# Expert rows gathered by quarters and turned by VectorE two tiles ahead, in a decoder layer with a grouped mixture of experts

## The reference, cut to what matters

```python
def chunk_fn(args):
    xc, gc = args
    h = jax.nn.silu(jnp.einsum('cd,edf->cef', xc, w_gate)) * jnp.einsum('cd,edf->cef', xc, w_up)
    h = h * gc[:, :, None].astype(h.dtype)
    return jnp.einsum('cef,efd->cd', h, w_down)
```

## Time and profile before

| | |
|---|---|
| median of 3 runs | 1026.58 us (1020.91 to 1030.8) |
| profiled execution | 1020.71 us; its span 1018.7 us |
| mean granted TensorE clock, whole span | 0.956 of full |
| TensorE matmuls | 909.4 us busy (89%) |
| VectorE | 687.5 us (67%) |
| ScalarE | 561.0 us (55%) |
| GpSimd | 366.0 us (36%) |
| expert tiles | from about 533 to 976 us of the span |

### The profile page before, as it was taken

The page is one execution under the profiler, slowest core; times in us unless marked ns, Lnnn a source line. Parts: engine busy times, 40 slices in busy tenths (PEclk is TensorE's granted clock), DMA queues, the critical chain, the costliest instruction groups (busy, mean ns, idle before and its releaser), DMA issues.

```text
span 1018.7 us, 15879 instructions
## 1 busy us (share of the span) xinstructions
PE 909.4 (89%) x4802; PEld 712.9 (70%) x4803; DVE 687.5 (67%) x1017; ACT 561.0 (55%) x804; POOL 366.0 (36%) x238
## 2 busy tenths in 40 slices
PE   6999999999897899999918999999999999999920
PEld 5877888644465567888717888888887888888710
DVE  4339888896999945737697748798888734314326
ACT  4256576787686665702334646777777634323323
POOL 0000089999999990000000212213323211111116
PEclk9999999999799999999959999999999999999965
DMA  8550111000000100433565889999999897433264
GB/s 232 128 144 21 42 42 63 1 1 1 1 2 1 43 1 22 156 124 148 234 249 207 294 285 313 405 382 404 399 388 405 305 352 226 125 65 99 41 198 173
DMA packets 63052, 171.15 MB, mean 168 GB/s; under 512 B 19200, under 2 KB 33536, under 8 KB 50688
## 3 DMA queue, kind: packets, MB, share of 16 engines
q1 hardware_dynamic: 55664, 143.85, 38.4%
q0 software_dynamic: 7056, 25.69, 10.6%
q10 hardware_dynamic: 288, 1.05, 0.3%
HBM read 141.74 MB, written 26.21 MB: 165 GB/s over the span
## 4 chain that ended last, share of the span: by engine, by line
PE 45%; DMA 10%; DVE 6%; ACT 2%; issue 2%; POOLq 0%; POOL 0%; ACTq 0%; DVEq 0%; SPq 0%
PE ps L459 13%; PE ps L461 12%; PE ps L460 12%; DMA raw<-in_w_gate 8%; PE ps L924 2%; PE ps L797 1%; DVE wlo L1708 1%; DVE sm L1549 1%; ACT whi L1215 1%; PE ps L764 1%; PE ps L960 1%; PE ps L848 1%; DMA acc_d<-ysb,idx_add 1%; PE ps L784 1%; DVE xa L1563 0%
## 5 line engine op out<-in xcount | busy, mean ns | idle before, releaser
L1708 DVE TENSOR_TENSOR wlo<-raw,whi 128x2048 fp32r<-128x2048 f32 x96 | 216.0, 2287 | 51.2 <-ACT whi L1215 51.1
L1215 ACT CAST whi<-raw 128x2048 fp32r<-128x2048 f32 x96 | 180.4, 1912 | 47.9 <-DMA raw<-in_w_gate 18.5
L459 PE MATMUL ps<-whi,xgT_hi 128*128 128x512 f32 x384 | 152.0, 396 | 5.4 <-DVE xgT_lo L1718 5.4
L461 PE MATMUL ps<-whi,xgT_lo 128*128 128x512 f32 x384 | 149.8, 390 | 0.0
L460 PE MATMUL ps<-wlo,xgT_hi 128*128 128x512 f32 x384 | 149.5, 389 | 0.0
L1803 POOL TENSOR_SCALAR tapped<-hpad,par 128x1024 f32<-128x1024 f32 x30 | 92.0, 3067 | 3.0
L459 PE MATMUL ps<-xT_hi,w_hi 128*128 128x512 f32 (+1 forms) x224 | 87.2, 389 | 4.7 <-DVE w_lo L1304 3.0
L459 PEld LDWEIGHTS ps<-whi,xgT_hi 128*128 128x128 f32 x384 | 72.3, 188 | 21.3 <-issue 5.6
L461 PE MATMUL ps<-xT_hi,w_lo 128*128 128x512 f32 (+1 forms) x224 | 86.3, 385 | 0.0
L460 PE MATMUL ps<-xT_lo,w_hi 128*128 128x512 f32 (+1 forms) x224 | 86.3, 385 | 0.0
L1881 POOL COPY idx_now<-slot_token 128x1 int32 (+1 forms) x24 | 7.7, 319 | 218.7 <-PE ps L924 218.7
(11 more groups left out here) (305 smaller groups left out, 1825.0 us busy)
## 6 DMA issues: line engine op xcount, KB each, us to landing
raw<-in_w_gate SPq DMA_DIRECT2D x32, 1024.0 KB
raw<-in_w_up SPq DMA_DIRECT2D x32, 1024.0 KB, 12.7
raw<-in_w_down SPq DMA_DIRECT2D x32, 1024.0 KB
w_raw<-in_w_in SPq DMA_DIRECT2D x14, 512.0 KB, 4.1
x_tok<-in_x SPq DMA_DIRECT2D x8, 512.0 KB, 7.4
wo_raw<-in_w_o SPq DMA_DIRECT2D x16, 256.0 KB, 3.0
x_res<-in_x SPq DMA_DIRECT2D x16, 256.0 KB, 3.4
x_d<-xa SPq DMA_DIRECT2D x4, 512.0 KB, 6.0
```

The source lines that it names most:

```text
L459: pe.matmul(out, l_hi, r_hi, start=start, stop=False)
L461: return pe.matmul(out, l_lo, r_hi, start=False, stop=stop)
L1215: act.copy(whi[:, n, :], raw[:, n, :]).then_inc(gu_hi if n < 4 else dn_hi, 1)
L1708: dve.tensor_tensor(wlo[:, n, :], raw[:, n, :], f32(whi[:, n, :]), ALU.subtract).then_inc(gu_lo if n < 4 else dn_lo, 1)
```

## The change

Each index table entry now leads to four quarter rows. `xg` has row quarter q of 32 tokens on partitions 32q to 32q+31, and the four groups of 32 tokens of a tile lie beside each other in it: four indirect DMAs of 128 x 1 KB in place of one of 128 x 4 KB. One VectorE instruction, in 32x32 blocks, turns `xg` into `xr`, a new SBUF buffer with the layout that the eight TensorE transposes gave in PSUM. `xr` is written for tile t+2 behind `h_lo_part(t)`, so the next fetch is for tile t+3; the `add_rows` of GpSimd now stands ahead of the `fetch` in its loop. Tile 0 is fetched and transposed as before. The index table `idx4` is made once: four small matmuls with `spread` and one VectorE instruction. `xr` lies where the last x1 tile lay, so its first write waits for `acc_out` and the read back of `acc_d` waits for its last use.

```diff
+        x1_quarters = x1_d.rearrange("r (q n) -> (r q) n", q=4)
+        def x_source(t):
+            return pair(2) if isinstance(t, int) and t == 0 else xr[:].rearrange("p k n -> p (k n)")
...
             sp.dma_start(ln2_b[:], a["ln2_b"][0].partition_broadcast(P)).then_inc(ln2_in, 16)
+            sp.wait_ge(xg_tr, last_t + 3)
             sp.wait_ge(y_out, last_t * 16 + 16)
...
-            def xgT(t):
-                pe.wait_ge(xg_in, t * 16 + 16)
+            pe.wait_ge(table_set, 2)
+            for t4 in range(4):
+                last = pe.matmul(ps[:, 6, P + 32 * t4:P + 32 * t4 + TILES + 1], spread[:, t4, :], spare_no,
+                                 start=True, stop=True)
+            last.then_inc(table_mm, 1)
+
+            def first_xgT():
+                pe.wait_ge(xg_in, 16)
...
             gate_up(0, 0)
-            xgT(1)
             hidT(0)
             def tile(t):
                 gate_up(t, loads(t))
-                xgT(t + 1)
                 down(t - 1, loads(t - 1))
                 hidT(t)
...
-                act.copy(xgT_hi[:].rearrange("p k n -> p (k n)"), pair(2)).then_inc(xgT_hi_s, 1)
+                act.copy(xgT_hi[:].rearrange("p k n -> p (k n)"), x_source(t)).then_inc(xgT_hi_s, 1)
...
             dve.tensor_tensor(slot_token[:], spare_no, filled, ALU.add).then_inc(table_set, 1)
+            dve.tensor_tensor(spare_no, spare_no, filled, ALU.add).then_inc(table_set, 1)
...
             last.then_inc(gate_hot, 1)
+            for q in range(4):
+                link(dve.memset(quarter_no[32 * q:32 * q + 32, :], float(q)))
+            dve.wait_ge(table_mm, 2)
+            dve.tensor_scalar(idx4[:, :, 0:TILES + 1], ps[:, 6, P:2 * P].rearrange("p (t n) -> p t n", t=4), 4.0,
+                              quarter_no[:], ALU.mult, ALU.add).then_inc(table_set, 1)
...
-                dve.tensor_tensor(xgT_lo[:].rearrange("p k n -> p (k n)"), pair(2),
+                dve.tensor_tensor(xgT_lo[:].rearrange("p k n -> p (k n)"), x_source(t),
                                   f32(xgT_hi[:]).rearrange("p k n -> p (k n)"), ALU.subtract).then_inc(xgT_lo_s, 1)
+            def x_turned(t):
+                dve.wait_ge(xg_in, t * 64 + 16)
+                if isinstance(t, int) and t == 1:
+                    dve.wait_ge(acc_out, 16 * NT)
+                else:
+                    dve.wait_ge(xgT_lo_s, t)
+                dve.transpose(xr[:].rearrange("p b (t j) -> p t b j", t=4), xg[:].rearrange("p (t i b) -> p t b i", t=4, b=KT)
+                              ).then_inc(xg_tr, 1)
...
             split_new(1, range(3))
+            x_turned(1)
             hidden(0)
             x_lo_part(1)
             split_new(1, [3])
             h_lo_part(0)
+            x_turned(2)
             split((4, 5), 0)
...
                 x_lo_part(t + 1)
                 split_new(t + 1, [3])
                 h_lo_part(t)
+                x_turned(t + 2)
                 split_new(t, (4, 5))
...
+            pool.tensor_copy(spread[:].rearrange("p t (q j) -> p t q j", q=4),
+                             ident[:].rearrange("p (t j) -> p t j", t=4).unsqueeze(2).to_broadcast([P, 4, 4, 32]))
+            pool.iota(idx4[:, :, TILES + 1:], [[0, 4], [0, 1]], 0, 1, **small).then_inc(rconst, 1)
...
             def fetch(t):
                 pool.wait_ge(xg_tr, t)
-                pool.tensor_copy(idx_now[:], slot_token[:, bass.ds(t, 1)]).then_inc(idx_set, 1)
+                pool.tensor_copy(idx_now[:].unsqueeze(2), idx4[:, :, bass.ds(t, 1)]).then_inc(idx_set, 1)
                 pool.wait_ge(x1_out, 16 * NT)
                 pool.wait_ge(idx_set, t)
-                pool.indirect_dma_start(xg[:], None, x1_d, bass.IndirectOffsetOnAxis(ap=idx_now[:], axis=0)
-                                        ).then_inc(xg_in, 16)
+                for t4 in range(4):
+                    pool.indirect_dma_start(xg[:, 256 * t4:256 * t4 + 256], None, x1_quarters,
+                                            bass.IndirectOffsetOnAxis(ap=idx_now[:, t4:t4 + 1], axis=0)).then_inc(xg_in, 16)
...
+            pool.wait_ge(table_set, 3)
             for t in range(1, 4):
                 fetch(t)
             add_rows(0)
-            with pool.Fori(4, TILES + 1) as t:
-                with pool.If(t <= last_t + 1):
+            fetch(4)
+            with pool.Fori(5, TILES + 2) as t:
+                with pool.If(t <= last_t + 2):
+                    add_rows(t - 4)
                     fetch(t)
-                    add_rows(t - 3)
```

More of the change, by code:

```diff
@@ L296, in program @@
         xgT_lo = at("xgT_lo", [P, KT, P], F32R, 200)
+        xr = at("xr", [P, KT, P], F32, R2 + 12)
+        idx4 = at("idx4", [P, 4, TILES + 2], I32, 77.25)
+        spread = at("spread", [P, 4, P], F32, 77.875)
+        quarter_no = at("quarter_no", [P, 1], F32, 79.875)
         silu = at("silu", [P, DE], F32, CST + 0.5)
@@ L374, in program @@
         slot_gate = at("slot_gate", [P, TILES + 1], F32, END + 0.125)
-        idx_now = at("idx_now", [P, 1], I32, END + 0.25)
+        idx_now = at("idx_now", [P, 4], I32, END + 0.25)
         idx_add = at("idx_add", [P, 1], I32, END + 0.3125)
@@ L906, in _ @@
             pe.wait_ge(oh_set, 1)
-            pe.wait_ge(rconst, 4)
+            pe.wait_ge(rconst, 5)
             for t in range(NT):
@@ L964, in _ @@
             last_t = pe.value_load(last_tile, min_val=MIN_TILES - 1, max_val=TILES - 1)
-            xgT(0)
+            first_xgT()
             pe.wait_ge(gate_hot, 1)
```

## The result

The changed kernel took 1055.9 us (median of 4 runs, 1050.1 to 1060.1) against 1026.3 us for the kernel before: a ratio of 1.029, 95% interval 1.021 to 1.036. It is slower, by some 30 us; I had forecast 1023.9, a range of 1013 to 1045, and a small gain. The profiled execution took 1060.1 us with a span of 1058.3, 39.6 us more than the span before. Where the executions of one kernel spread by more than 1.5%, its ratio counts only those within 1.5% of its fastest, which flatters it, so the median and the range of all stand beside it. The kernel before, run beside each of them, stays within 1020.9 to 1031.8.

The account below looks back on a forecast made before the run. TensorE was taken to bound start and end, full DMA engines the middle. End -7.9, start -1.8, prologue +4.0 and small gathers +3.0 gave -2.7 us: 1018.0 profiled, 1023.9 us by the median, whole range 1013 to 1045.

Parts of the forecast that it names:

- The end stretch: Tiles 16 to 23, TensorE-bound: nine transpose groups of 0.88 us leave the path, 7.9 us gained, tiles of 16.87 us.
- DMA cost of the small gathers: DMA-full middle, about ten tiles: four gathers of 1 KB pieces take 0.3 us more each, +3.0 us (0 to +7).
- the queue rival: Middle tiles: small gather packets alternate singly with weight packets, rows land late, about +17 us, 1044 by the median; chance 0.28.
- VectorE as the bound: Rival, middle tiles: a VectorE transpose over 2.7 us uses up its gaps; at 3.5 us, +8 us, 1032 by median; chance 0.08.
- the cheaper start: Rival, prologue: shorter waits and small packets costing only their bytes, -10.2 to -11.5 us, 1016 by the median; chance 0.19.
- The transpose: One VectorE transpose per tile: 1.3 us (1.2 to 1.8), hidden in VectorE's gaps, no cost to the time.
- The strided row: Profile row behind the transpose estimate: a strided VectorE read took 622 ns against 420 contiguous, a factor 1.5.
- GpSimd's timetable: Middle tiles: index copy and gathers each get in per split, rows land at about 17 of 18.5 us, hidden, 1.5 spare.
- The prologue: Tiles 1 and 2 at the start: fetch(2) waits for tile 1's turn, gate-up of tile 2 later, +4 us (-1.8 to +6).
- The sum: Whole kernel: -7.9 - 1.8 + 4.0 + 3.0 = -2.7 us, a ratio of 0.9974, 1023.9 us by the median.

Follow-up runs that it names:

- e12: Changed kernel with a second gather buffer, index cell and semaphore, and VectorE held for the index copy between the two down splits: 1018.9 us, ratio 0.993.
- e1: Changed kernel, with VectorE waiting behind each of its transposes until GpSimd has copied the next tile's indices: 1043.0 us, ratio 1.018.
- e6: Changed kernel, with VectorE's transpose reading xg contiguously instead of at a stride (rows in wrong order): 1017.1 us, ratio 0.994.
- e8: Kernel before the change, its one gather released at the end of h_lo instead of TensorE's transposes, scatter-add ahead of it: 1069.2 us, ratio 1.044.
- e10: Changed kernel with the transpose reading contiguously, plus a second contiguous transpose of three quarters of the tile into an unread buffer: 1027.3 us, ratio 1.0015.
- e11: Changed kernel, one gather buffer, with VectorE held for the index copy between the two down splits: 1039.4 us, ratio 1.008.
- e2: Changed kernel, with VectorE copying the indices itself ahead of its transpose and GpSimd only gathering: 1046.4 us, ratio 1.025.
- e3: Changed kernel with one gather of 4 KB rows in place of four of 1 KB (rows in wrong layout): 1037.1 us, ratio 1.008.
- e5: Changed kernel with a second gather buffer, index cell and semaphore for odd tiles, so gathers may start one tile earlier: 1034.6 us, ratio 1.000.
- e7: Changed kernel with two gather buffers and the gathers released by VectorE's hid instead of its transpose: 1026.6 us, ratio 0.999.
- e9: Changed kernel with two gather buffers, gathers released by VectorE's hid and put ahead of the scatter-add: 1060.1 us, ratio 1.036.

## Why the prediction was wrong

**The end stretch** was right: 7.9 us forecast for nine tiles, 7.3 measured over eight of them, tiles of 16.83 us (forecast 16.87).

**DMA cost of the small gathers**, +3.0 us: wrong, it is nothing. In e12, whose middle is bound by the transfers (DMA share 1.02 to 1.03), the tiles take 18.48 to 18.59 us as in the kernel before, with four gathers each. q0 has 8400 packets where it had 7056: 25 x 4 x 48 - 24 x 144 = 1344. So a gather of 128 pieces of 1 KB shows as 48 records, 32 packets of 4096 B and 16 semaphore writes: four pieces travel together. That is the rule of the Trainium skill's page "DMA: Bandwidth & Descriptors", section "SWDGE vs HWDGE vs iDMA", that the prediction cites. That also disposes of the queue rival, to which I had given 0.28. It forecast the right sign and over half of the loss (1044) by a mechanism that is not there. Both of its signs were seen all the same: middle tiles over 19.5 us with VectorE waiting for `xg`, and the packets of the software queue spread, 192 in 767 to 776.4 for one tile. They are spread because the four gathers are issued over 9 us (762.61 to 771.43), so the sign didn't tell this rival from GpSimd's lateness. VectorE as the bound (0.08) is not what holds the changed kernel either, with 58.4 us of waiting, but it holds e1; the cheaper start (0.19) did not come.

**The transpose**, 1.3 us: wrong, 2.15. The step that failed is "nearer to the plain pass, because the stride here is 32 bytes and there 128". The strided row had a factor of 1.5; the measured one is 1.7 over the plain 1.24.

**GpSimd's timetable** is the step on which the forecast broke: "the index copy gets in behind the first down split, 3.6; then one gather per split [...] landed at about 17", with 1.5 us to spare. Two things failed in it. Where the copy does get in (759.79), the rows land 18.9 us after the transpose's start, 1.9 us later than forecast: 0.9 of it is the transpose and 0.8 the issues, the last of which took 1.89 us where I had counted 1.0. There was nothing to spare. And in four middle tiles of this profile it did not get in for the whole chain, which in one of them put landing at 25.9 us (669.80 to 695.68). I had read "during a split GpSimd gets in only at its end" from single gathers of 1.00 and 2.28 us. But in the kernel before these were released by TensorE, at a time when no chain of five splits followed. The rows bounded the price of meeting one split; I used them for meeting five. That use holds in e6, e8 and e10, where the copy or gather gets in at the first end each time; it fails only behind the strided transpose, which no row of the kernel before could show.

The Trainium skill, page "SBUF — State Buffer", section "A bandwidth-pool intuition that's wrong (but worth ruling out)", has the blocked side go on some 115 ns after VectorE's instruction ends, measured there on a DMA of the software queue beside a copy on VectorE. The copies that are let in fit that in kind (in e12 the split ends at 744.32, the copy at 744.38); the one at 672.18, past four ends of splits, does not, and the measurement decides.

**The prologue**, +4: the mechanism was right, fetch(2) waits for the turn of tile 1. Without a shut-out (e6) it cost +5.7 us; in the changed kernel +13.7, since the copy at 564.70 was shut out for 10.96 us and tile 2's gate and up follow from it.

**The sum.** With the shut-out gone, the forecast's sum comes out: e6, whose transpose costs 1.24 us where I had assumed 1.3, has a span 3.3 us below that of the kernel before, where I had forecast -2.7, and 1017.1 us in the median. That it is so near is partly luck: the prologue cost 1.7 us more than its term, and the 3.0 us of the small gathers weren't there. The loss of the changed kernel therefore lies in the step on GpSimd's timetable, 33.5 us in the middle and about 8 of the prologue. Of the 33.5, e11, with nobody shut out in the middle but the ring too long, keeps 13.0; the other 20 or so came with the four shut-outs. Both shares hold for these two profiled executions, and include some of the half clock behind each stall.

Open: why a copy that starts at the same place in the same chain is let in at one tile and not at the next, and why this was seen only behind the strided read and only without a gap.

## What to carry to other kernels

Before a wait is put in front of a run of back-to-back VectorE instructions with two SBUF inputs, ask which GpSimd instruction it releases: price that one at the whole run, not at one instruction, where a strided read runs straight into it (23 of 59 here, none of 70 elsewhere), and ask what is queued behind it. A price read from single encounters doesn't cover a run. Where the release can't move, a hold inside the run (0.17 us) and one more buffer cost less than a hold ahead of it (2.0 us).

## What the runs showed of the hardware

- GpSimd's copy of 128x4 integers takes 0.19 us alone, 2.07 behind one split and 10.87 when shut out for five. All 23 instructions over 8 us in the profiles here (5, 4, 4, 4, 3, 2 and 1 in the changed kernel, e2, e3, e5, e7, e9 and e11) began within 1.2 us of the start of a chain of four or five splits that followed a strided transpose without a gap, and ended with the chain or within 0.9 us behind it; the 36 others that began there, and all 70 at chains behind a contiguous transpose or an idle VectorE, took at most 3.03 us.
- A 32x32-block transpose of 128x1024 float32 on VectorE: 1.24 us read contiguously, 2.15 us at a stride of 32 bytes.
- Four gathers of 128 pieces of 1 KB take the same DMA time as one of 4 KB rows: q0 is busy 10.7% of 1015 us in e6, 108.6 us, where 24 gathers and as many scatter-adds before took 10.6% of 1019, 108.0 us.
- From the end of its issue the last gather landed 1.85 us later with the DMA engines otherwise idle (560.59 to 562.44) and 4.0 to 4.9 us later in the full stretch.
